# Folded sums of the squared-ReLU activations in the down projection: VectorE instead of GpSimd

## The reference

```
def mlp_sq_relu(hn, w_up, w_down):
    return jnp.square(jax.nn.relu(hn @ w_up)) @ w_down

h = h + mlp_sq_relu(rmsnorm(h, norm_mlp[i]), w_up[i], w_down[i])     # w_up 1024x4096, w_down 4096x1024
```

## Time and profile before

| | |
|---|---|
| median of 3 runs | 2630.05 us (2629.63 to 2631.31) |
| the profiled execution | 2628.29 us |
| its span (first to last instruction) | 2626.7 us |
| PE busy | 2526.7 us (96%), 11896 matmuls |
| DVE busy | 1892.2 us (72%), 2562 instructions |
| ACT busy | 1145.4 us (44%) |
| POOL busy | 798.6 us (30%), 586 instructions |
| GpSimd's folded sums on `hid_raw` | 120, 196.6 us, 1647 ns each |

### The profile page before, as it was taken

How to read it: one execution, slowest core, us unless ns; L and a number is a source line. 1 busy time by engine, 2 the same in 40 slices (tenths; PEclk the granted TensorE clock), 3 DMA queues, 4 the chain that set the end, 5 groups by cost and what they waited for, 6 DMA issues and landing times.

```text
span 2626.7 us, 32491 instructions
## 1 busy us (share of the span) xinstructions
PE 2526.7 (96%) x11896; PEld 2078.6 (79%) x11896; DVE 1892.2 (72%) x2562; ACT 1145.4 (44%) x1862; POOL 798.6 (30%) x586
## 2 busy tenths in 40 slices
PE   7999999899999999999999999989999998999998
PEld 6878888787888778887778888878788886888777
DVE  7677655657666789998765657665766668999876
ACT  6555433535444444444442324353534444444343
POOL 2000000023323466666320000002423236666642
PEclk9999999999999999999999999999999999999999
DMA  3100000122333432322221011012233333323112
GB/s 131 32 26 25 26 31 25 49 80 101 108 114 108 132 113 97 128 97 72 73 96 41 25 33 39 25 41 88 96 117 106 111 132 103 122 97 125 62 56 81
DMA packets 78640, 207.64 MB, mean 79 GB/s; under 512 B 8672, under 2 KB 10736, under 8 KB 78496
## 3 DMA queue, kind: packets, MB, share of 16 engines
q1 hardware_dynamic: 75552, 195.85, 22.5%
q0 software_dynamic: 2224, 7.54, 0.8%
q10 hardware_dynamic: 720, 2.36, 0.2%
HBM read 163.25 MB, written 42.47 MB: 78 GB/s over the span
## 4 chain that ended last, share of the span: by engine, by line
PE 67%; issue 16%; DVE 12%; ACT 4%; POOL 1%; DMA 0%; POOLq 0%; DVEq 0%; ACTq 0%; SPq 0%
PE gemm_ps L743 9%; PE gemm_ps L745 9%; PE gemm_ps L744 9%; PE s_ps L743 8%; PE s_ps L745 7%; PE s_ps L744 7%; PE to_ps L745 5%; PE to_ps L744 5%; PE to_ps L743 5%; DVE wlo L2315 1%; DVE b_blocks_lo L2402 1%; DVE wlo L1917 1%; PE to_ps L849 1%; ACT prob L1436 1%; DVE a_blocks L2402 1%
## 5 line engine op out<-in xcount | busy, mean ns | idle before, releaser
L743 PE MATMUL gemm_ps<-a_hi,whi 128*128 128x512 f32 x1024 | 424.6, 415 | 21.9 <-DVE a_lo L1926 11.9
L745 PE MATMUL gemm_ps<-a_hi,wlo 128*128 128x512 f32 x1024 | 403.1, 394 | 0.0
L744 PE MATMUL gemm_ps<-a_lo,whi 128*128 128x512 f32 x1024 | 402.0, 393 | 0.0
L743 PEld LDWEIGHTS gemm_ps<-a_hi,whi 128*128 128x128 f32 x1024 | 194.4, 190 | 62.2 <-issue 21.7
L745 PEld LDWEIGHTS gemm_ps<-a_hi,wlo 128*128 128x128 f32 x1024 | 193.6, 189 | 43.1
L1251 POOL TENSOR_TENSOR hid_raw<-hid_raw 128x512 f32<-128x512 f32 x120 | 196.6, 1647 | 99.2 <-DVE a_blocks L2402 33.1
L744 PEld LDWEIGHTS gemm_ps<-a_lo,whi 128*128 128x128 f32 x1024 | 194.4, 190 | 32.8 <-issue 1.4
L2315 DVE TENSOR_TENSOR wlo<-wraw_a,whi 128x512 fp32r<-128x512 f32 (+1 forms) x204 | 180.3, 885 | 32.1 <-ACT whi L1607 31.1
L2315 DVE TENSOR_TENSOR wlo<-wraw,whi 128x512 fp32r<-128x512 f32 (+1 forms) x204 | 180.1, 884 | 32.2 <-ACT whi L1607 31.8
L1607 ACT ACTIVATE whi<-wraw_a 128x512 fp32r<-128x512 f32 (+1 forms) x204 | 122.6, 602 | 182.3 <-PE s_ps L745 137.3
L743 PE MATMUL s_ps<-b_blocks_hi,whi 128*128 128x512 f32 x448 | 178.3, 398 | 16.9 <-DVE wlo L2315 10.3
(11 more groups left out here) (390 smaller groups left out, 6378.1 us busy)
## 6 DMA issues: line engine op xcount, KB each, us to landing
wraw<-panels SPq DMA_DIRECT2D x90, 512.0 KB, 3.6
wraw<-folds SPq DMA_DIRECT2D x60, 512.0 KB, 4.3
wraw_a<-folds SPq DMA_DIRECT2D x60, 512.0 KB, 4.3
hid_raw<-hidden SPq DMA_DIRECT2D x120, 256.0 KB, 3.7
hidden<-sumsq SPq DMA_DIRECT2D x64, 256.0 KB, 2.6
hidden<-zs SPq DMA_DIRECT2D x32, 256.0 KB, 2.1
hidden<-zt SPq DMA_DIRECT2D x32, 256.0 KB, 2.0
h<-x_t SPq DMA_DIRECT2D x11, 512.0 KB, 5.3
```

The source lines that it names most:

```text
L743: nc.tensor.matmul(out, hi_w, hi_x, start=start, stop=False, skip_group_check=True)
L744: nc.tensor.matmul(out, hi_w, lo_x, start=False, stop=False, skip_group_check=True)
L745: return nc.tensor.matmul(out, lo_w, hi_x, start=False, stop=stop, skip_group_check=True)
```

## The change

VectorE makes the folded sums T1 to T4 of all 16 pairs in both layers (`first_sum`), each right behind the `lo` of the block that it waited for, and counts them in a semaphore of its own. `FIRST_PAIRS = SUBS` (16) makes the condition `s < FIRST_PAIRS` true for all pairs. GpSimd passes over them. The operands, the places and the operation are the same. The helper `t_made` now returns the semaphore with the count.

```diff
+FIRST_PAIRS = SUBS
...
         def t_made(layer, s, name):
-            return 4 * (SUBS * layer + s) + T_COUNT[name]
+            if s < FIRST_PAIRS:
+                return t_first_ready, 4 * (FIRST_PAIRS * layer + s) + T_COUNT[name]
+            return t_ready, 4 * ((SUBS - FIRST_PAIRS) * layer + s - FIRST_PAIRS) + T_COUNT[name]
+
+        def t_parts(s, name):
+            b11, b12, b21, b22 = (hid_src(s, x) for x in ("B11", "B12", "B21", "B22"))
+            return {"T1": (b11, b12, b11), "T3": (b12, b12, b22), "T2": (b11, b22, b11), "T4": (b21, b21, b11)}[name]
...
                 def x_sums(n, j):
                     for s, i in taken_in(n, j):
+                        if s < FIRST_PAIRS:
+                            continue
                         if i == 0:
                             x_sum(s, "T1")
...
+                def first_sum(s, name):
+                    if name == "T1":
+                        dve.wait_ge(*hid_loaded(layer, s, "B12"))
+                    if name == "T3":
+                        dve.wait_ge(*hid_loaded(layer, s, "B22"))
+                    if name == "T4":
+                        dve.wait_ge(*t_made(layer, s, "T2"))
+                    out, in0, in1 = t_parts(s, name)
+                    V.tensor_tensor(out, in0, in1, ALU.subtract).then_inc(t_first_ready, 1)
+
                 def hid_lo(s, j):
                     hi, lo = hid_block(s, j)
                     dve.wait_ge(hid_hi_ready, taken_at(layer, s, j))
                     V.tensor_tensor(lo, hid_src(s, X_BLOCK[j]), hi, ALU.subtract).then_inc(hid_lo_ready, 1)
+                    if s < FIRST_PAIRS:
+                        for made, name in ((0, "T1"), (1, "T3"), (1, "T2"), (2, "T4")):
+                            if made == j:
+                                first_sum(s, name)
```

More of the change, by code:

```diff
@@ L458, in build_trunk @@
         second_loaded = {name: sem("second_loaded_" + name) for name in B_RAW}
+        t_first_ready = sem("t_first_ready")
         t_ready, hid_hi_ready, hid_lo_ready = sem("t_ready"), sem("hid_hi_ready"), sem("hid_lo_ready")
@@ L686, in load_hidden @@
                         sp.wait_ge(hid_lo_ready, taken_at(layer, ahead, X_BLOCK.index("T2")))
-                        sp.wait_ge(t_ready, t_made(layer, ahead, "T4"))
+                        sp.wait_ge(*t_made(layer, ahead, "T4"))
                     else:
@@ L1236, in x_sum @@
                 def x_sum(s, name):
-                    b11, b12, b21, b22 = (hid_src(s, x) for x in ("B11", "B12", "B21", "B22"))
                     if name == "T1":
@@ L1242, in x_sum @@
                         gp.wait_ge(*hid_loaded(layer, s, "B22"))
-                        gp.wait_ge(t_ready, t_made(layer, s, "T1"))
+                        gp.wait_ge(*t_made(layer, s, "T1"))
                     if name == "T2":
@@ L1247, in x_sum @@
                         gp.wait_ge(hid_lo_ready, taken_at(layer, s, X_BLOCK.index("B21")))
-                        gp.wait_ge(t_ready, t_made(layer, s, "T2"))
-                    out, in0, in1 = {"T1": (b11, b12, b11), "T3": (b12, b12, b22), "T2": (b11, b22, b11),
-                                     "T4": (b21, b21, b11)}[name]
+                        gp.wait_ge(*t_made(layer, s, "T2"))
+                    out, in0, in1 = t_parts(s, name)
                     nc.gpsimd.tensor_tensor(out, in0, in1, ALU.subtract).then_inc(t_ready, 1)
@@ L1664, in hid_hi @@
                     else:
-                        act.wait_ge(t_ready, t_made(layer, s, name))
+                        act.wait_ge(*t_made(layer, s, name))
                     A(hi, hid_src(s, name), ACT.Copy).then_inc(hid_hi_ready, 1)
```

## The result

The changed kernel takes 2651.79 us (median of 5 runs, 2646.07 us at the least), the one before 2630.05. One of the five was a disturbed run of 5310 us and stays out of the comparison. The ratio is 1.0083, with an interval of 1.0066 to 1.0100: 0.8% slower. Forecast were 2621.6 us, with a range from 2614 to 2631. The profiled execution took 2651.17 us, its span is 2649.6.

The account below looks back on a forecast made before the run. TensorE, 96% busy, was taken as the bound, waiting at the starts on VectorE's queue. Gains of 2 x 3.2 + 2 x 1.0 = 8.4 us take the profiled 2628.3 to 2619.9; the median, 1.8 above, is 2621.6 us, range 2614 to 2631.

Parts of the forecast that it names:

- The starts: Start of each layer's down projection: VectorE's waits for ScalarE go and TensorE gains 3.2 us per layer.
- the refund: VectorE time given back per folded sum taken from GpSimd: about 0.6 us, range 0.3 to 1.1, leaving VectorE's work unchanged.
- The price per folded sum: Each folded sum adds 0.60 us to VectorE's queue and is recorded with 0.68 to 0.69.
- The folded sums themselves recorded far over 0.7 us: Sign that would show the forecast wrong: VectorE's own folded sums taking far longer than 0.7 us.
- The signs of being right: At each start: VectorE busy 55 to 58 us, its waits for ScalarE about 2 us, TensorE's busy time up about 3.
- The waits on loads: VectorE's sums T1 and T3 waiting for loads: taken as 0, bound 0.4 us for each of 6 odd pairs.
- The waits that VectorE gets: Step on waits new in VectorE's queue, with weight splits and a PSUM addition behind them: priced at 0.
- The middle: Twelve later pairs per layer: 28.8 us added to VectorE and 28.8 taken away; TensorE gains 1.0 us per layer (0 to 2.3).
- VectorE has 27 us in hand: Slack of VectorE in the down projection's middle, busy 233 of 260 us, cited against harm from load waits.
- GpSimd's own queue gets free as well: At the starts, weight sums and ScalarE's work come earlier; nothing added, 1.5 us kept for the low end.
- The slower one: Rival: remaining weight sums cost 1.1 us each and VectorE becomes the bound, at starts and middles: 2645 us, chance 0.09.
- its mean of 0.6 us per GpSimd sum: Average VectorE slowdown per GpSimd sum in the down projection, 0.59 to 0.64 us, under half of a full hold.

Follow-up runs that it names:

- the paced kernel: The changed kernel, with GpSimd in turns 20 to 30 waiting for the odd pair's T4 before the next turn's S1: 2618.93 us, ratio 0.9954.

## Why the prediction was wrong

**The starts held, with a size off.** The gain was put at 3.2 us per layer and is 4.7 and 3.9. VectorE's waits for ScalarE in front of the blocks of the pairs fall from 5.0 to 2.7 us in the fixed window, which by now also holds a wait of 1.1 us from further on. Its splits from `hid_raw` into `b_blocks_lo` take 683 ns instead of 1034 as a mean:

```profile
L2424 DVE TENSOR_TENSOR a_blocks<-hid_raw,a_blocks 128x512 fp32r<-128x512 f32 x14 | 11.1, 793 | 1.2 <-ACT a_blocks L1677 1.2
L2419 DVE TENSOR_TENSOR hid_raw<-hid_raw 128x512 f32<-128x512 f32 x12 | 10.1, 864 | 0.0
L2424 DVE TENSOR_TENSOR b_blocks_lo<-hid_raw,b_blocks_hi 128x512 fp32r<-128x512 f32 x7 | 4.7, 683 | 1.5 <-ACT b_blocks_hi L1677 1.5
```

Between the same two VectorE instructions (at 892.17 and 954.71 us before, 894.65 and 951.18 after) the stretch shrinks from 62.5 to 56.5 us. These waits fall in it from 5.0 to 1.7 us, 3.4 less, as good as the 3.2 of the prediction. VectorE's busy time falls by 2.3 us (1.5 in layer 1), where the prediction had no change. TensorE gets 4.7 of the 6.0. So the mis-sized term is the refund. It was taken as 0.6 us per folded sum; here it is (9.6 + 2.3) / 16 = 0.75, in layer 1 0.70. In the middle of the paced kernel 48 sums more (28.8 us) come with 5.7 us less busy time: 34.5 / 48 = 0.72 each. This lies inside the bounds of 0.3 to 1.1; the value taken was low.

**The price per folded sum held.** 0.60 us from start to start, 0.68 to 0.69 recorded, where no GpSimd sum lies beside it. Beside one it does not: the 48 folded sums of the middle are recorded with 0.82 us as a mean, and T3 of turn 22 with 1.77. "The folded sums themselves recorded far over 0.7 us" was a sign of being wrong in the prediction, and at the place that matters it came. The signs of being right came as well (VectorE busy for 57.7 and 56.5 us at the starts, TensorE by 3.0 and 5.2 more): they all look at the starts.

**The waits on loads did not hold, in a small part.** They were taken as 0, with a bound of 0.4 us. In the middle of layer 0 VectorE waits twice for a load in front of T1, for 0.76 and 0.67 us, just ahead of turns 20 and 26. In these two turns TensorE waits 2.02 and 2.03 us for bank A, and 0.32 and 0.22 shortly before, where the other four have 1.77. In the paced kernel the same two waits are 1.05 and 1.04 us, and it is in the same two turns that TensorE still waits 0.73 and 0.71 us. Its third wait, 0.83 us in turn 30 of layer 1, comes after ScalarE waited 1.22 us for a load. No run changes the loads alone, so this is read from the rows.

**The step that failed is "The waits that VectorE gets", and with it "The middle",** which was put at a gain of 1.0 us per layer and lost 15.5 and 15.9. The step named "the PSUM addition that TensorE needs one block later" as queued behind the new instructions, and then priced only the loads that they might wait for. It did not add up the instructions themselves: T3 and T2 put 1.2 us in front of a read that had 1.0 us in hand in turn 22 (it ends at 1022.73, block 2 starts at 1023.90, and 0.15 us lie between them in the changed trace), and only 0.3 in turn 20. It answered with an average, "VectorE has 27 us in hand", for a deadline that comes once in two turns. An average of 215.9 of 260 us busy goes together with a loss of 15 us here.

The second half of the failure is in "GpSimd's own queue gets free as well", which was booked at nothing, or as a gain at the low end of the range. In the paced kernel the read comes only 0.42 us later than before (3.81 against 3.39 us): the 1.2 us of the two sums are mostly paid by the splits, which no folded sum on GpSimd slows any more. This fits into what is in hand but for the waits of 0.7 to 0.8 us in 3 of 12 turns. The 2.1 us of S1 and S3, which moved to where the slowed instructions are, do not. The code says that these two are held back in even turns (`later`), but it does so by their place in a queue behind folded sums, and the change took these away.

**The sum after the fact.** Layer 0's middle: six times two matmuls start 2.15 to 2.42 us apart instead of 0.23, which gives 12.1. (The waits as recorded, 1.77 to 2.03, are shorter, as a recorded matmul reaches into the gap.) Two slices of 3.4 us at half clock follow such waits:

```profile
986.10:989.50 3.40, 3.40 (x10) 2.63 (x9) 3.40 (x6) 0.42 (x1) 0.00 (x0) 0.50 0.00 0
1109.00:1112.40 3.40, 3.40 (x9) 2.65 (x8) 3.31 (x6) 0.26 (x1) 0.00 (x0) 0.51 0.00 0
```

Nine or ten matmuls in 3.4 us instead of 15 cost 1.1 to 1.4 us each. That makes 14.6 of the 15.5; of the rest, 0.5 are the two shorter waits named above. In layer 1 there are three such slices. In the kernel with only T2 behind the read (waits of 1.17 to 1.42 us) no slice at half clock lies in a middle, nor in the kernels without the waits. The changed kernel has 5 in its first trace and 4 in its second, of some 1.2 us each. These are most of the other half of the 13 us between the two kernels.

**The rivals.** The slower one gave 2645 us, near the measured time, by a mechanism that isn't this one: weight sums at 1.1 each *everywhere* would fill VectorE, and would make each start 6 us longer, where it got shorter. In the paced kernel the 62 GpSimd sums of the middle cost (227.5 - 331 x 0.60) / 62 = 0.47 each, less than before. The 1.07 is right only for sums that meet a VectorE instruction with two SBUF inputs near their beginning.

The Trainium skill ("SBUF — State Buffer", section "Who interferes with whom") calls the pair of ports that VectorE and GpSimd share an exclusive lock. The prediction set its mean of 0.6 us per GpSimd sum against this, and that was a misreading: taken one by one, the instructions agree with the rule. The first split above ends 0.55 us after S4 ends (1022.48 and 1021.93), the second 0.56 after S1 (1024.17 and 1023.61), T3 0.55 after S3 (1025.86 and 1025.31). In the two down projections of the kernel before, 214 VectorE instructions on two 128x512 SBUF tiles start while a GpSimd sum still has 0.15 us or more to go. All 214 last until 0.55 us (0.54 to 0.56) after its end. What a GpSimd sum costs VectorE is thus what is left of it when such an instruction comes. That is up to 1.1 us here, and nothing as far as VectorE reads PSUM meanwhile; a mean of 0.6 says nothing against a hold of the whole 1.3.

## What to carry to other kernels

Before moving work into an in-order queue, take each instruction behind it that another engine needs soon, and count what stands in front of it, slowed as it will be there, against the time until it is needed, at the worst place of the schedule; a busy share says nothing on this. And ask what the removed work held back on the engine that it left: an instruction without a wait of its own may have been timed by its neighbours in the queue. Here one semaphore wait for GpSimd, in six turns of each layer, makes the difference between 0.8% slower and 0.5% faster.

## What the runs showed of the hardware

A VectorE instruction on two 128x512 SBUF tiles that starts inside a GpSimd sum is held until that sum ends: it lasts until 0.55 us after the sum's end (214 of 214 in the down projections of the kernel before). VectorE instructions with one input from PSUM are not held: 126 of them overlap a GpSimd sum there by more than 0.5 us, and all are recorded with 0.67 to 0.69. In the mean a GpSimd sum of two 128x512 float32 tiles cost VectorE 0.47 us in the middle of the paced kernel, and 1.07 in front of the late read; on 16 columns it cost about 0.02 there ((3.85 - 3.81) / 2). A GpSimd sum that meets VectorE's work is stretched itself, from 1.29 to 1.74 us.

In the middles of the two traces of the changed kernel, TensorE's ten waits recorded with 1.91 to 2.03 us were followed by a 3.4 us slice at a granted clock of 0.5, the lower of the two levels, in nine cases. The 14 waits of 1.77 or 1.78 us never were, nor the 12 of 1.17 to 1.42 us in the kernel with T2 behind the read. Nothing here separates the length of the wait from its place.
